# Down projections of the second block: eight of 22 feature tiles as seven block products, in three of four pairs of output tiles

## What is computed

```
def swiglu(x, w_gate, w_up, w_down):
    return (jax.nn.silu(x @ w_gate) * (x @ w_up)) @ w_down
...
        h = h + 0.5 * swiglu(rmsnorm(h, ffn1_norm[l]), ffn1_w_gate[l], ffn1_w_up[l], ffn1_w_down[l])
...
        h = h + 0.5 * swiglu(rmsnorm(h, ffn2_norm[l]), ffn2_w_gate[l], ffn2_w_up[l], ffn2_w_down[l])
```

## Time and profile before

| | |
|---|---|
| median of 3 runs | 3070.7 us (3069.38 to 3071.08) |
| the profiled execution, as timed | 3069.67 us |
| its span in the profile | 3068.0 us |
| PE, DVE, ACT, POOL busy | 99%, 66%, 46%, 6% |
| matmuls | 20304 |

### The profile page before, as it was taken

One profiled execution on the slowest core, in us unless ns is written; L12 is line 12 of the kernel. 1 busy time (PEld: TensorE's weight loads), 2 busy tenths in 40 slices (PEclk: granted clock), 3 DMA queues, 4 the chain that ended last, 5 costly groups with the idle time before them and its releaser, 6 DMA issues.

```text
span 3068.0 us, 55404 instructions
## 1 busy us (share of the span) xinstructions
PE 3040.7 (99%) x20304; PEld 2760.2 (90%) x20304; DVE 2026.5 (66%) x3009; ACT 1411.0 (46%) x2481; POOL 171.6 (6%) x213
## 2 busy tenths in 40 slices
PE   9999999999999999999999999999999999999998
PEld 7778887788888799999999999999999999889987
DVE  5545545773576488855667788747886566778864
ACT  4454434442343365633752455525553375255642
POOL 1000000000000011100000011001110000001100
PEclk9999999999999999999999999999999999999999
DMA  4111322222222267532211477335762222247723
GB/s 161 62 65 59 110 89 98 89 93 96 92 95 96 82 157 182 144 103 90 69 63 56 130 189 175 99 97 168 175 160 90 96 70 70 65 143 190 174 96 109
DMA packets 121793, 341.30 MB, mean 111 GB/s; under 512 B 13774, under 2 KB 13774, under 8 KB 121536
## 3 DMA queue, kind: packets, MB, share of 16 engines
q1 hardware_dynamic: 97776, 292.33, 28.9%
q0 software_dynamic: 23600, 46.87, 9.2%
q10 hardware_dynamic: 288, 0.31, 0.0%
HBM read 337.29 MB, written 2.17 MB: 111 GB/s over the span
## 4 chain that ended last, share of the span: by engine, by line
PE 72%; issue 23%; DVE 3%; ACT 1%; POOL 1%; DVEq 0%; POOLq 0%; DMA 0%; ACTq 0%
PE ps L2187 29%; PE ps L2308 9%; PE ps L2578 8%; PE ps L2575 8%; PE ps L2576 8%; PE ps L2860 3%; PE ps L2325 1%; PE ps L2393 1%; PE ps L2641 1%; PE ps L2251 0%; PE ps L2362 0%; PE ps L2381 0%; PE ps L2286 0%; DVE xT L1383 0%; DVE w_lo L1326 0%
## 5 line engine op out<-in xcount | busy, mean ns | idle before, releaser
L708 ACT ACTIVATE w_hi<-w_raw 128x1024 fp32r<-128x1024 f32 x352 | 372.7, 1059 | 784.9 <-PE ps L2187 562.5
L1326 DVE TENSOR_TENSOR w_lo<-w_raw,w_hi 128x1024 fp32r<-128x1024 f32 x360 | 440.1, 1222 | 337.4 <-ACT w_hi L708 331.6
L2187 PE MATMUL ps<-f_hi,w_hi 128*128 128x264 f32 (+1 forms) x1488 | 383.7, 315 | 0.0
L2187 PE MATMUL ps<-f_lo,w_hi 128*128 128x264 f32 (+1 forms) x1488 | 383.4, 315 | 0.0
L2187 PE MATMUL ps<-f_hi,w_lo 128*128 128x264 f32 (+1 forms) x1488 | 382.4, 314 | 0.0
L2187 PE MATMUL ps<-h_hi,w_hi 128*128 128x512 f32 (+1 forms) x832 | 275.1, 359 | 4.7 <-DVE w_lo L1326 4.6
L2187 PE MATMUL ps<-h_lo,w_hi 128*128 128x512 f32 (+1 forms) x832 | 274.3, 358 | 0.0
L2187 PE MATMUL ps<-h_hi,w_lo 128*128 128x512 f32 (+1 forms) x832 | 273.0, 356 | 0.0
L2187 PEld LDWEIGHTS ps<-f_hi,w_hi 128*128 128x128 f32 x1488 | 244.3, 188 | 18.8
L2187 PEld LDWEIGHTS ps<-f_hi,w_lo 128*128 128x128 f32 x1488 | 244.0, 188 | 18.3
L2187 PEld LDWEIGHTS ps<-f_lo,w_hi 128*128 128x128 f32 x1488 | 244.7, 188 | 17.3
(11 more groups left out here) (423 smaller groups left out, 7511.7 us busy)
## 6 DMA issues: line engine op xcount, KB each, us to landing
w_raw<-in_stream SPq DMA_DIRECT2D x436, 512.0 KB, 3.3
s_raw<-in_stream SPq DMA_DIRECT2D x152, 256.0 KB, 4.3
s_raw<-in_stream POOLq DMA_DIRECT2D x152, 256.0 KB, 4.2
tmp<-in_stream SPq DMA_DIRECT2D x76, 256.0 KB, 5.0
xT<-in_x POOLq DMA_DIRECT2D x1, 2048.0 KB, 9.5
out<-h_spare SPq DMA_DIRECT2D x8, 256.0 KB, 2.2
xT<-in_x SPq DMA_DIRECT2D x7, 256.0 KB, 5.7
const<-in_const POOLq DMA_DIRECT2D x1, 1636.0 KB, 9.6
```

Source lines behind the costliest of these rows:

```text
L708: nc.scalar.activation(w_hi[:, s, :], w_raw[:, s, :], ACT.Copy).then_inc(hi_done, 1)
L1326: V.tensor_tensor(w_lo[:, s, :], w_raw[:, s, :], w_hi[:, s, :].bitcast(F32), ALU.subtract).then_inc(lo_done, 1)
L2187: last = T.matmul(out[:, p, :], w[:, s, j * P:(j + 1) * P], x[:, k, c0:c1], start=start and j == 0 and r == 0, stop=stop and j == len(ks) ...
```

## The change

Output tiles 0 and 1 stay plain, in seven smaller units (0 to 6) that take feature tiles 0-7, 16-21 and 8-15 in that order. Each of the pairs of tiles (2, 3), (4, 5) and (6, 7) becomes seven units (7 to 13, 14 to 20, 21 to 27). Four are plain: P0, P1 and P2 of 8 feature tiles each, W with 4 plain tiles and one block product. Three, called A, S and Q, hold two block products each, so each pair has seven of them (12 matmuls each), on feature tiles 8-15. Their weights come from a new buffer, w_mix, which three more loads of SP per pair fill, to which two POOL loads add, and in which DVE makes two sums. New on DVE are four sums of f2 blocks and their lower parts, new on ACT their upper parts. Per pair, ACT copies three banks out of PSUM, DVE makes two small combinations (`second_chain`, `last_chain`), and a tile's result is now a sum of PSUM and the copies, scaled in an instruction of its own. The waits for a bank to be free stand at the unit that writes it first. In the last call the plain units of the three pairs also run as two matmuls of 256 columns. All of it is unrolled. The order of the work around it does not change.

The core of the diff:

```
+N_DOWN = 28
+D_FIRST = KT
+D_PAIRS = KT // 2 - 1
...
+D_ORDER = {1: ["P0", "P1", "P2", "W", "A", "S", "Q"],
+           2: ["P0", "P1", "A", "S", "Q", "W", "P2"],
+           3: ["A", "S", "Q", "W", "P0", "P1", "P2"]}
+D_PLAIN = {"P0": [(0, k) for k in range(8)], "P1": [(0, k) for k in range(16, 22)] + [(1, 16), (1, 17)],
+           "P2": [(1, k) for k in range(8)], "W": [(1, k) for k in range(18, 22)]}
+D_FIRST_PAIR = [(0, range(0, 8)), (1, range(0, 8)), (0, range(16, 22)), (1, range(16, 22)),
+                (0, range(8, 16)), (1, range(8, 12)), (1, range(12, 16))]
+F_ORDER = [*range(0, 8), *range(16, 22), *range(8, 16)]
...
+        D_MIXED = {"A": slice(1, 3), "S": slice(0, 2), "Q": slice(2, 4)}
...
+                def mixed_loads(p):
+                    sp.dma_start(w_mix[:, 0, :], stream_d[unit_of(2 * p + 1, 1), :, BLK:]).then_inc(s1_base[1], 16)
+                    sp.dma_start(w_mix[:, 3, :], stream_d[unit_of(2 * p, 1), :, 0:BLK]).then_inc(s3_base[1], 16)
+                    sp.dma_start(d_mixed("A"), stream_d[unit_of(2 * p, 1), :, :]).then_inc(wg_in[1], 16)
...
+                for d in range(2, N_DOWN):
+                    s, p, kind = d % 2, d // 7, d_kind(d)
+                    if d == 4:
+                        sp.wait_ge(product_done, 7 * (win_first(which, L) + N_WIN))
+                        mixed_loads(1)
+                    sp.wait_ge(lo_done, down + d - 1)
+                    if kind in D_MIXED:
+                        sp.sem_inc(w_arrived[s], 16)
...
+                    elif kind == "P1":
+                        sp.dma_start(w_raw[:, s, 0:6 * P], stream_d[unit_of(2 * p, 2), :, 0:6 * P]).then_inc(w22_in[1], 16)
+                        sp.dma_start(w_raw[:, s, 6 * P:], stream_d[unit_of(2 * p + 1, 2), :, 0:2 * P]).then_inc(w_arrived[s], 16)
+                    elif kind == "W":
+                        sp.dma_start(w_raw[:, s, 0:BLK], stream_d[unit_of(2 * p + 1, 1), :, BLK:]).then_inc(w22_in[1], 16)
+                        sp.dma_start(w_raw[:, s, BLK:], stream_d[unit_of(2 * p + 1, 2), :, 2 * P:6 * P]).then_inc(w_arrived[s], 16)
...
+                    for p in range(1, D_PAIRS):
+                        if d == d_at(p, "Q") + 2:
+                            mixed_loads(p + 1)
...
+                for p in range(1, D_PAIRS + 1):
...
+                    pool.dma_start(w_mix[:, 0, :], w21, accum_op=ALU.add).then_inc(s1_in[1], 16)
...
+                    pool.dma_start(w_mix[:, 3, :], w21, accum_op=ALU.add).then_inc(s3_in[1], 16)
...
+                def d_next(d):
+                    kind = d_kind(d + 2) if d + 2 < N_DOWN else "plain"
+                    if kind not in D_MIXED:
+                        if kind in ("P1", "W"):
+                            act.wait_ge(w22_in[1], d_landed22(which, L, (d + 2) // 7, kind))
+                        split_hi(*following(u0 + FF2_TILES + d // 2, d % 2), BLK if d in (3, 4) else KT * P)
+                        return
+                    Z = E0 + N_WIN + (d + 2) // 7 - 1
+                    if kind == "A":
+                        act.wait_ge(wg_in[1], d_landed(which, L, (d + 2) // 7))
+                    else:
+                        act.wait_ge(win_sum, Z + 1)
+                    if kind == "Q":
+                        act.wait_ge(s3_in[1], d_landed(which, L, (d + 2) // 7))
+                    act.wait_ge(unit_done, down + d + 1)
+                    nc.scalar.activation(w_hi[:, d % 2, :], d_mixed(kind), ACT.Copy).then_inc(hi_done, 1)
+                def d_copy_out(slot, bank_no, scale=1.0):
+                    nc.scalar.activation(cp[:, slot, :], ps[:, bank_no, 0:hn], ACT.Copy, scale=scale).then_inc(copied, 1)
...
+                for k in range(16, 22):
+                    f_upper(k)
+                d_next(0)
+                for k in range(8, 16):
+                    f_upper(k)
+                d_next(1)
+                for n in range(2):
+                    d_t_upper(n)
+                d_next(2)
+                for n in range(2, 4):
+                    d_t_upper(n)
+                for d in range(3, 7):
+                    d_next(d)
+                for p in range(1, D_PAIRS + 1):
+                    for d in range(7 * p, 7 * p + 7):
+                        if d == d_at(p, "A"):
+                            act.wait_ge(slot_free[0], g0 + FF2_TILES + p)
+                            act.wait_ge(product_done, 7 * (E0 + N_WIN + p - 1) + d_product(p, "w11"))
+                            d_copy_out(0, 6)
+                        if d == d_at(p, "S"):
+                            act.wait_ge(slot_free[1], g0 + FF2_TILES + p)
+                            act.wait_ge(product_done, 7 * (E0 + N_WIN + p - 1) + d_product(p, "s1"))
+                            d_copy_out(3, 7, -1.0)
+                        if d == d_at(p, "Q"):
+                            act.wait_ge(unit_done, down + d + 1)
+                            d_copy_out(2, 6, -1.0)
+                        d_next(d)
+                        if p == D_PAIRS and d == d_at(p, "W") and not last:
+                            for k in range(2 * D_PAIRS):
+                                act.wait_ge(sumsq_done, sums0 + k + 1)
+                                h_upper(q, k, q + 2, T2)
+                        if p == D_PAIRS and d >= 7 * p + 5 and not last:
+                            act.wait_ge(slot_free[d - 7 * p - 5], g0 + FF2_TILES + D_PAIRS + 1)
+                            h_upper(q, 2 * D_PAIRS + d - 7 * p - 5, q + 2, T2)
...
+                    V.tensor_tensor(t1, b11, b12, ALU.subtract).then_inc(t_sum, 1)
+                    V.tensor_tensor(t3, b22, b12, ALU.subtract).then_inc(t_sum, 1)
+                    dve.drain()
+                    V.scalar_tensor_tensor(t2, t1, -1.0, b22, ALU.mult, ALU.subtract).then_inc(t_sum, 1)
+                    between()
+                    dve.drain()
+                    V.tensor_tensor(t4, b21, t2, ALU.add).then_inc(t_sum, 1)
...
+                def d_next(d):
...
+                    dve.wait_ge(hi_done, down + d + 3)
+                    V.tensor_tensor(w_lo[:, d % 2, :], d_mixed(kind), w_hi[:, d % 2, :].bitcast(F32), ALU.subtract
+                                    ).then_inc(lo_done, 1)
+                    if kind == "A":
+                        dve.drain()
+                        dve.wait_ge(s1_in[1], d_landed(which, L, (d + 2) // 7))
+                        V.tensor_tensor(w_mix[:, 1, :], w_mix[:, 0, :], w_mix[:, 1, :], ALU.add)
+                        dve.drain()
+                        V.tensor_tensor(w_mix[:, 2, :], w_mix[:, 1, :], w_mix[:, 2, :], ALU.add).then_inc(win_sum, 1)
...
+                def take(m, y, inc=True):
+                    x = tile(xT, m, n_tok)
+                    step = V.scalar_tensor_tensor(x, y, 0.5, x, ALU.mult, ALU.add)
+                    if inc:
+                        step.then_inc(slot_free[m % 2], 1)
+                    new_x(q, m, x, n_tok, last or m < 2 * D_PAIRS)
+                def d_out(p, s, between=None):
+                    y = tmp[:, 2, 0:n_tok]
+                    base = d_banks(which, L, p)[s]
+                    step = V.tensor_tensor(y.rearrange("p (a n) -> p a n", a=2), ps[:, base:base + 2, 0:hn],
+                                           cp[:, 2 * s:2 * s + 2, :], ALU.add)
+                    if p < D_PAIRS:
+                        step.then_inc(slot_free[s], 1)
+                    if between is not None:
+                        between()
+                    dve.drain()
+                    V.tensor_tensor(y, y, rstd[:, 0:n_tok], ALU.mult)
+                    dve.drain()
+                    take(2 * p + s, y, inc=p == D_PAIRS)
...
+                for k in range(16, 22):
+                    f_lower(k)
+                d_next(0)
+                d_t_sums(lambda: d_next(1))
+                for k in range(8, 12):
+                    f_lower(k)
+                d_next(2)
+                for k in range(12, 16):
+                    f_lower(k)
+                for n in range(4):
+                    d_t_lower(n)
+                    if n == 2:
+                        d_next(3)
+                d_next(4)
+                d_next(5)
+                first_out(0)
+                d_next(6)
+                first_out(1)
+                def second_chain(p):
+                    Z = E0 + N_WIN + p - 1
+                    dve.drain()
+                    dve.wait_ge(unit_done, down + d_at(p, "S") + 1)
+                    dve.wait_ge(copied, 4 * Z + 2)
+                    V.tensor_tensor(cp[:, 1, :], ps[:, 6, 0:hn], cp[:, 3, :], ALU.subtract).then_inc(copied, 1)
...
+                def last_chain(p):
...
+                    dve.wait_ge(copied, 4 * Z + 4)
+                    V.tensor_tensor(cp[:, 3, :], cp[:, 3, :], cp[:, 2, :], ALU.add)
+                    dve.drain()
...
+                for d in range(7, 12):
+                    d_next(d)
+                second_chain(1)
+                d_next(12)
+                last_chain(1)
```

(60 more changed lines are left out.)

246 lines of the change are left out of this document (160 added, 86 removed).

## The result

The changed kernel takes 3080.19 us in the median of seven runs (3079.38 to 3082.96), the kernel before 3070.70 on the same chip (3069.38 to 3071.34): ratio 1.0034, 95% interval 1.0024 to 1.0044. It is slower, by 9.5 us, where the prediction had 5.0 and put "the same" (0.45) a little above "slower" (0.43). By the prediction's own measure (0.2%, 6.1 us) that is "slower". The profiled execution took 3080.19 us, 10.5 more than that of before.

The account below looks back on a forecast made before the run. PE was taken to bound the kernel, busy 3040.7 of 3068.0 us, any new wait costing its full length. 3 x 0.3 + 4.1 = 5.0 us slower gave 3075.7 us, range 3066 to 3085.

Parts of the forecast that it names:

- What goes: Matmuls saved in the down projections: 4.4 us per call with 528 tokens, 2.3 in the last, 15.5 without any wait.
- (d): Between S and W of the last pair, W's split stands behind tile 5's output on DVE: PE stands 2.1 us.
- (b): Before S: two DVE sums of weights follow A's split, so S's split comes late: PE waits 1.0 us.
- (e): The next stage's first weights are split behind tile 6's output, longer than P2 covers: PE waits 0.25 us.
- (c): W of pair 4, 5 loads in two parts once S is split: PE waits 0.2 us.
- (a): Before A (unit 16): its split stands behind two tile outputs, with P1's load 0.7 late: PE stands 1.1 us.
- rival 3: P1's load isn't delayed, so (a) falls to 0.4 us and the time to 3072.9 us; chance 0.08.
- The last call: Last down projection: 2.3 us saved against 5.75 of waits; with 0.6 at the kernel's end, 4.1 us slower.
- 0.3 two units on: Last call, two units after unit 5, where PE stands 0.8 us for DVE's work: a further wait of 0.3 us.
- Rival 4: PE's clock falls in a stand, once per call at 1.7 us: 3082.5 us; chance 0.03.
- Rival 2: DVE's chains end before PE needs them, so all 15.5 us come: 3055 us, with half 3063; chance 0.12.

Follow-up runs that it names:

- the rearranged order: The changed kernel with only DVE's order rearranged, several splits moved ahead of output operations, w_mix loads left in place: 3057.39 us, ratio 0.9959 to the kernel before.
- run 2: Two runs on the changed kernel: W's split of the last pair before tile 5's four remaining output operations, 3069.50 us; or one operation earlier, 3072.91 us.
- 3: The changed kernel with one more DVE operation of 0.69 us before W's split of the last pair: 3086.88 us, ratio 1.0057 to the kernel before.

## Why the prediction was right and wrong

The time fell inside the range (3066 to 3085), with an error of 4.5 us. But the loss of 9.5 us is nearly twice the 5.0 of the sum, and that it isn't further off is partly luck, as errors cancel: the waits of calls 1 to 3 were set too large, the last call's waits on loads too small, and the clock at nothing. The trace lets each term be read.

**What goes.** 20556 matmuls, as worked out. That 4.4 us go per call is shown by the rearranged order, where nothing stands and 4.2 are gained.

**(d), 2.1 us: right**, 2.04 to 2.07 in all four calls. Moving one line removes it (run 2), adding a step lengthens it (3), moving the split by one step cuts it to 1.25 (2). The order written for DVE is the cause.

**(b), 1.0 us: right in kind, a little high.** 0.61 to 0.82, and 0.91 in the last call. **(e), 0.25: right**, 0.23 to 0.27. **(c), 0.2: did not appear.**

**(a), 1.1 us: wrong through one choice.** I took P1's load as 0.7 late because three loads stand behind it. It landed after 3.1 us; the wait is 0.33, near the 0.4 of rival 3, which had 0.08. The up stage's 4.7 against 3.4 was the wrong row to lean on. The rule of the Trainium skill, DMA: Bandwidth & Descriptors, Queues, rings and completion order, that each DMA engine takes a queue's descriptors in the order of the ring, agrees with call 1's rows: 3.1 for what came first, 4.6 and 5.9 for what came behind. It doesn't tell the last call, where all of them were slow.

**The last call: missed by 3.7 us** (7.1 for 3.45). Its waits sum to 7.2 us where I had 5.75, and 2.0 of slow matmuls come on top. Unit 5's 0.53 stands for 0.8. The step that failed is "0.3 two units on": it took the load to be in time. Unit 7 waited 1.82 us and A 1.90, both with loads that took 5.1 and 4.5 us. Such landings come and go: at unit 7 3.3 and 4.6 in two other traces in which nothing ahead of it in that call was changed. PE waited at unit 7 in five of the ten traces in which the last call is changed (1.09 to 1.82 us), the five in which an instruction transfer began beside its load, and never there in the first three calls. The prediction left these transfers out altogether; against late loads it had only that memory is busy for 0.31 of the time. That the last call suffers more because its units are shorter while a load and DVE's work are not is likely and was not tested; a late load shows in call 3 too, 0.90 us at unit 14.

**Rival 4, the clock: right as a mechanism, with a far too small chance.** I gave it 0.03 since a stand of 1.4 us had left the clock at 1.00 and only one of "several us" had not the earlier trace rows. That was read wrongly from the kernel before. The second stand is one of 2.44 us and, after a few small matmuls, one of 0.62; and at 504 to 507 us the clock fell (0.51) behind a stand of 1.49 us, again with small matmuls between. So my own longest wait, 2.1 us, four times a run, was not short. PE's timeline and that window:

```profile
502.01 1.05 PE L2203 MATMUL ps<-params,norm_work 128*128 128x1 f32 x8 [1.49 <-DVE norm_work L1600]
...
504.00:507.50 3.50, 3.38 (x11) 2.54 (x11) 1.24 (x3) 0.00 (x0) 0.00 (x0) 0.51 0.47 150
...
1058.06 1.05 PE L2203 MATMUL ps<-params,norm_work 128*128 128x1 f32 x8 [2.44 <-DVE norm_work L1359]
```

In the profile of after it happened in three of four calls at 1.6 us each, near the 1.7 I had priced. Taken together, 4.8 of the 10.5 us. Without it calls 1 to 3 would have come to -1.4 us in sum, where I forecast +0.9: my waits were a little too large, and the clock more than made up for it. The clock goes with the spread too, run by run. The four executions of the changed kernel with a mean granted clock of 0.996 took 3079.38 to 3080.19 us, the three with 0.995 took 3082.18 to 3082.96. The kernel before, timed 66 times beside the runs, took 3069.36 to 3069.93 us in the 26 executions with 0.998 and 3070.43 to 3072.39 in the 40 with 0.997. The Trainium skill, TensorE: Matmul & The Clock Gate, Part 1: The HAM clock gate, has activity as what lifts the clock; that the stretch vanishes when the stand is filled, with W starting at the same time, agrees.

**Rival 2, the waits do not appear**, was wrong for this kernel, and right for what could be written: with another order for DVE 13.4 of the 15.5 us came in the medians, 12.3 in the profiled spans.

## What to carry to other kernels

When work units get shorter, write down for each what must be ready and what stands ahead of it on the engine that prepares it; a preparation that the critical engine waits for belongs ahead of operations that nobody waits for, even in the middle of a chain. Here that order alone was worth 22.8 us, the slow stretches of the clock included, more than the 15.5 of the matmuls saved. Price a stand of TensorE not only at its length, but also at the slow stretch that may follow, and check the shortest units (here the last call's) by themselves, with slow landings. When a loop is unrolled, look at the instruction queue in the DMA view as well: loads beside its transfers took up to 5.5 us here, for 3.3.

## What the runs showed of the hardware

- The granted clock can halve behind a stand of about 2 us. In the down projections of twelve traces (the changed kernel and the eleven runs), 19 stands of PE lasted 1.86 us or more, and behind 10 of them some 16 matmuls ran 0.22 us apart instead of 0.12, beginning 0.35 to 1.44 us after PE had resumed. Of the stands of 0.9 to 1.82 us none was followed by that. Among the longer ones length didn't decide: the clock stayed behind one of 2.33 and one of 3.02 us and fell behind one of 1.94. The bound holds for these stretches of full matmuls alone: at 502 us, where small matmuls follow a stand of some 1.5 us, the clock fell within 2.7 us of its end in ten of thirteen traces.
- A full-precision filler matmul of 512 columns takes 0.86 us in two records 0.43 apart, seven times the 0.12 of one of 264 columns in the split form.
- The same load at the same place of the program landed after 3.3, 4.6 and 5.1 us in three executions. All 73 lone 512 KB loads that took over 4.0 us had a 16 KB transfer of the instruction queue begin within 3 us of their issue; the 939 without one near them took 3.7 us at most.
